# Loads of block tiles issued from ScalarE's queue instead of SyncE's, in an fp32 two-layer kernel built on seven-product block matmuls

## The reference

```python
# first layer: D_FF = 8192
m = rms_norm(h, mlp_pre_gain[l])
z = jnp.square(jax.nn.relu(jnp.einsum("bsd,df->bsf", m, w_up[l])))
z = jnp.einsum("bsf,fd->bsd", z, w_down[l])
h = h + rms_norm(z, mlp_post_gain[l])
...
# second layer: D_FF_2 = 5632
h2 = rmsnorm(x, g_ffn)
gu = h2 @ w_gu
x = x + (jax.nn.silu(gu[..., :D_FF_2]) * gu[..., D_FF_2:]) @ w_down
```

## Time and profile before

| what | value |
|---|---|
| median of 3 runs | 2445.73 us (2445.54 to 2446.38) |
| the profiled execution's own time | 2447.08 us |
| its span in the trace | 2445.2 us |
| PE busy | 2437.5 us (100%) |
| DVE busy | 1818.0 us (74%) |
| ACT busy | 1486.3 us (61%) |
| DMA queue of SP | 66.8% of 16 engines' time |
| granted TensorE clock | 1.0 in all of it |

### The profile page before, as it was taken

One profiled execution on the slowest core, in us unless ns is written; L12 is line 12 of the kernel. 1 busy time (PEld: TensorE's weight loads), 2 busy tenths in 40 slices (PEclk: granted clock), 3 DMA queues, 4 the chain that ended last, 5 costly groups with the idle time before them and its releaser, 6 DMA issues.

```text
span 2445.2 us, 28786 instructions
## 1 busy us (share of the span) xinstructions
PE 2437.5 (100%) x10849; PEld 2017.9 (83%) x10849; DVE 1818.0 (74%) x1967; ACT 1486.3 (61%) x1801; POOL 66.8 (3%) x78
## 2 busy tenths in 40 slices
PE   9999999999999999999999999999999999999999
PEld 8888888888888888888888888888888888888887
DVE  5888578878888887766577645546688888878874
ACT  6886557567467576556666555546666545564553
POOL 0110000000000000011100000000000000000000
PEclk9999999999999999999999999999999999999999
DMA  8997667768678577576756666667767666675755
GB/s 283 267 262 219 197 197 206 230 201 228 215 207 243 189 230 208 153 219 211 228 179 200 196 202 199 202 193 215 242 189 217 212 198 216 197 223 182 229 175 172
DMA packets 348562, 515.41 MB, mean 211 GB/s; under 512 B 113840, under 2 KB 114152, under 8 KB 348168
## 3 DMA queue, kind: packets, MB, share of 16 engines
q1 hardware_dynamic: 343592, 496.63, 66.8%
q0 software_dynamic: 4688, 16.93, 3.2%
q10 hardware_dynamic: 144, 0.01, 0.0%
HBM read 476.52 MB, written 4.47 MB: 197 GB/s over the span
## 4 chain that ended last, share of the span: by engine, by line
PE 92%; DVE 4%; ACT 2%; issue 1%; DMA 1%; SPq 0%; POOL 0%; DVEq 0%; ACTq 0%; POOLq 0%
PE acc L601 15%; PE acc L603 15%; PE acc L602 15%; PE acc L766 12%; PE acc L767 12%; PE acc L768 12%; DVE w_lo L1554 2%; PE acc L754 1%; PE acc L755 1%; PE acc L753 1%; PE tp L754 1%; PE tp L755 1%; PE tp L753 1%; PE sc L753 1%; PE sc L754 1%
## 5 line engine op out<-in xcount | busy, mean ns | idle before, releaser
L1554 DVE TENSOR_TENSOR w_lo<-raw,w_hi 128x1024 fp32r<-128x1024 f32 x776 | 941.6, 1222 | 496.4 <-ACT w_hi L970 490.8
L970 ACT ACTIVATE w_hi<-raw 128x1024 fp32r<-128x1024 f32 x776 | 814.9, 1057 | 723.9 <-PE acc L603 378.8
L601 PE MATMUL acc<-w_lo,a_hi 128*128 128x512 f32 x1216 | 476.9, 392 | 0.7 <-issue 0.7
L603 PE MATMUL acc<-w_hi,a_lo 128*128 128x512 f32 x1216 | 473.8, 390 | 0.0
L602 PE MATMUL acc<-w_hi,a_hi 128*128 128x512 f32 x1216 | 473.5, 389 | 0.0
L767 PE MATMUL acc<-w_hi,a_hi 128*128 128x512 f32 x816 | 317.6, 389 | 0.0
L766 PE MATMUL acc<-w_lo,a_hi 128*128 128x512 f32 x816 | 317.6, 389 | 0.0
L768 PE MATMUL acc<-w_hi,a_lo 128*128 128x512 f32 x816 | 317.6, 389 | 0.0
L970 ACT ACTIVATE w_hi<-quad_raw 128x1024 fp32r<-128x1024 f32 x196 | 207.7, 1060 | 112.1 <-PE acc L768 60.2
L601 PEld LDWEIGHTS acc<-w_lo,a_hi 128*128 128x128 f32 x1216 | 228.4, 188 | 48.0 <-issue 1.7
L603 PEld LDWEIGHTS acc<-w_hi,a_lo 128*128 128x128 f32 x1216 | 228.3, 188 | 47.9
(11 more groups left out here) (310 smaller groups left out, 2881.6 us busy)
## 6 DMA issues: line engine op xcount, KB each, us to landing
raw<-w_in_dram SPq DMA_DIRECT2D x272, 512.0 KB, 4.6
raw<-w_down_dram SPq DMA_DIRECT2D x172, 512.0 KB, 4.4
raw<-w_gu_dram SPq DMA_DIRECT2D x136, 512.0 KB, 4.5
raw<-w_up_dram SPq DMA_DIRECT2D x100, 512.0 KB, 4.5
raw<-w_out_dram SPq DMA_DIRECT2D x64, 512.0 KB, 4.4
quad_raw<-w_down_dram SPq DMA_DIRECT2D x44, 512.0 KB, 6.1
quad_raw<-w_gu_dram SPq DMA_DIRECT2D x40, 512.0 KB, 5.6
raw<-w_branch_dram SPq DMA_DIRECT2D x32, 512.0 KB, 4.1
```

Source lines behind the costliest of these rows:

```text
L601: nc.tensor.matmul(out, xh, wl, start=s == 0 and k == 0, stop=False)
L603: mm = nc.tensor.matmul(out, xl, wh, start=False, stop=s == n - 1 and k == KS - 1)
L970: nc.scalar.activation(w_hi[:, g % RING], src, ACT.Copy).then_inc(hi_ready, 1)
L1554: nc.vector.tensor_tensor(w_lo[:, g % RING], src, w_hi[:, g % RING].bitcast(F32), ALU.subtract).then_inc(lo_ready, 1)
```

## The change

The 112 loads of block tiles leave SP's program and go into ACT's, each behind the rounding of a slot of the pair that runs. For a following pair that starts at slot `G_PAIR`, tile 1 is issued 10 slots earlier (index 9 of the running pair), tile 0 nine earlier (index 10), tile 2 seven earlier (index 12) and tile 3 four earlier (index 15). The waits are the same semaphores and values, taken by ACT. Sources, tiles and sizes stay; the order of the tiles was 1, 0, 3, 2 and is 1, 0, 2, 3. SP keeps the plain loads and the transposes. The source function moves out of SP's program unchanged.

```diff
+LOAD_AT = {G_PAIR[name] + i: (tile, q) for q, name in enumerate(QUADS)
+           for tile, i in ((1, -10), (0, -9), (2, -7), (3, -4))}
...
         @block.sync
...
-            def load_block(q, tile, src):
-
-                if q == 0:
-                    sp.wait_ge(slot_used, G_MLP)
-                    sp.wait_ge(h_ready, NCH)
-                elif q == Q_FF:
-                    sp.wait_ge(slot_used, G_FF)
-                else:
-                    g, order = G_PAIR[QUADS[q - 1]], DOWN if "down" in QUADS[q - 1][0] else UP
-                    last = ("T2", "T3", "B21", "B22")[tile]
-                    sp.wait_ge(lo_ready, g + order.index(last) + 1)
-                    sp.wait_ge(quad_sum, 4 * q)
-                sp.dma_start(quad_raw[:, tile], src).then_inc(quad_in[tile], 16)
...
-                blocks = {6: 1, 8: 0, 10: 3, 11: 2}
...
                     load(pair_src(name, unit, s))
-                    if following in QUADS and k in blocks:
-                        tile = blocks[k]
-                        load_block(QUADS.index(following), tile, pair_src(following, tile % 2, tile // 2))
...
         @block.scalar
         def _(act):
+            def load_block(tile, q):
+
+                if q == 0:
+                    act.wait_ge(slot_used, G_MLP)
+                    act.wait_ge(h_ready, NCH)
+                elif q == Q_FF:
+                    act.wait_ge(slot_used, G_FF)
+                else:
+                    g, order = G_PAIR[QUADS[q - 1]], DOWN if "down" in QUADS[q - 1][0] else UP
+                    last = ("T2", "T3", "B21", "B22")[tile]
+                    act.wait_ge(lo_ready, g + order.index(last) + 1)
+                    act.wait_ge(quad_sum, 4 * q)
+                act.dma_start(quad_raw[:, tile], pair_src(QUADS[q], tile % 2, tile // 2)
+                              ).then_inc(quad_in[tile], 16)
...
                 nc.scalar.activation(w_hi[:, g % RING], src, ACT.Copy).then_inc(hi_ready, 1)
+                if g in LOAD_AT:
+                    load_block(*LOAD_AT[g])
```

More of the change, by code:

```diff
@@ L389, in tap_first, with pair_src @@
                                         cols[:, G_CBIAS + c:G_CBIAS + c + 1], ALU.mult, ALU.add)
+        def pair_src(name, unit, s):
+            stage, b, i = name
+            if stage == "up":
+                c0 = b * D + (2 * i + unit) * W
+                return w_up[:, slice(KS * s, KS * s + KS), c0:c0 + W]
+            if stage == "down":
+                c0 = (2 * i + unit) * W
+                return w_down[:, b * KT + KS * s:b * KT + KS * s + KS, c0:c0 + W]
+            if stage == "ff down":
+                c0 = (2 * i + unit) * W
+                return w_dn2[:, b * KT + KS * s:b * KT + KS * s + KS, c0:c0 + W]
+            c0 = unit * FF2 + b * D + i * W
+            return w_gu[:, slice(KS * s, KS * s + KS), c0:c0 + W]
         block = ctx.enter_context(nc.Block())
@@ L460, in _, with load_pair @@
                     load(w_out[:, ks(part * RING + s), c0:c0 + W])
-            def load_block(q, tile, src):
-                if q == 0:
-                    sp.wait_ge(slot_used, G_MLP)
-                    sp.wait_ge(h_ready, NCH)
-                elif q == Q_FF:
-                    sp.wait_ge(slot_used, G_FF)
-                else:
-                    g, order = G_PAIR[QUADS[q - 1]], DOWN if "down" in QUADS[q - 1][0] else UP
-                    last = ("T2", "T3", "B21", "B22")[tile]
-                    sp.wait_ge(lo_ready, g + order.index(last) + 1)
-                    sp.wait_ge(quad_sum, 4 * q)
-                sp.dma_start(quad_raw[:, tile], src).then_inc(quad_in[tile], 16)
[L476 to L491, removed]
-                blocks = {6: 1, 8: 0, 10: 3, 11: 2}
+            def load_pair(name, turns):
                 if name in QUADS:
@@ L498, in load_pair @@
                     steps = [(unit, s) for unit in range(2) for s in range(SPU)]
-                    blocks = {k + 3: tile for k, tile in blocks.items()}
                 for k, (unit, s) in enumerate(steps):
@@ L503, in load_pair @@
                     load(pair_src(name, unit, s))
-                    if following in QUADS and k in blocks:
-                        tile = blocks[k]
-                        load_block(QUADS.index(following), tile, pair_src(following, tile % 2, tile // 2))
             mlp_pairs = [(stage, b, i) for b in range(MLP_BLOCKS) for stage in ("up", "down")
                          for i in range(2)]
-            for name, following in zip(mlp_pairs, mlp_pairs[1:] + [None]):
+            for name in mlp_pairs:
                 stage, b, i = name
@@ L517, in _ @@
                     turns = {3: [("ff", x + 2)], 8: [("ff", x + 3)]}
-                load_pair(name, following, turns)
+                load_pair(name, turns)
             for v in range(3 * NCH):
@@ L550, in _ @@
                         [("ff", b, j) for j in range(FF_PAIRS[b])] + [("ff down", b, i) for i in range(2)]]
-            for name, following in zip(ff_pairs, ff_pairs[1:-1]):
+            for name in ff_pairs:
                 stage, b, j = name
```

## The result

| | us, median (lowest to highest) |
|---|---|
| before | 2446.06 (2445.54 to 2446.41, 4 runs) |
| after | 2476.06 (2468.89 to 2483.97, 4 runs) |

The ratio is 1.0122, with an interval of 1.0110 to 1.0134: slower by 30.0 us. The forecast was 2447.5, at most 2449.3 at the end of its range. The prediction was wrong. The profiled execution is the fastest of the four after, 2468.89 us, with a span of 2467.1; the time to explain in the trace is 2467.1 - 2445.2 = 21.9 us.

What follows compares the result with a forecast made beforehand. PE was taken as the bound, busy 2437.5 of 2445.2 us. Two tight pairs at +0.9 us, all else 0, gave +1.8 us on 2445.73: 2447.5 us, with an 8-in-10 range of 2444.9 to 2449.3.

Steps and rivals of the forecast that it cites:

- The bound, the tight pairs, the path: PE bounds; in two `ff down` pairs (0.15 us slack) a later transpose delays join, remainder and PE's matmul one for one.
- SP loses 112 issues: SP's queue: without the block load ahead, transposes go out up to 0.5 us earlier in each of two pairs.
- ACT gains 112 issues: ACT's queue, four issues a pair at about 0.42 us: taken as 0, upper end 0.5 us in all.
- ACT's new waits: ACT waiting for the T4 sum ahead of tile 1: taken as 0, at most under one DVE operation, 1.22 us.
- Rival B: Block-load issues on ACT held about 4 us by full engines: 90 us slower, 2535 us; chance 0.05.
- The tiles arrive at other times: Block tiles' landing: tile 3 has 11.3 us, slowest landing 8.9, 2.4 us left, so no new wait.
- The first pair: Join at 364.35, tile 3 moving beside its transposes: taken as 0, estimated -1 to +1 us.
- Tile 2 moves ahead of the transposes' end: Tile 2 goes out during the transposes: -0.5 to +1.5 us per tight pair with the earlier issue, +0.9 taken.
- In these two pairs, and only in them with certainty: Only in `("ff down", 0, 0)` and `("ff down", 1, 0)` does a later transpose certainly delay PE, one for one.
- Rival C: Transposes delayed by tiles 0 and 2 in three pairs, 3.0 us each: +7.5 us, 2453.2 us; chance 0.04.
- The 2.0 us that I drew from it: Cost for the two tight pairs if tile 2 is served within the transposes by turns: 2 x (1.5 - 0.5).

Runs made afterwards that it cites:

- experiment 8: The kernel before, all on SP's queue, with tile 0 issued behind the transposes instead of ahead of them in the second layer's pairs: 2444.64 us, ratio 0.9993.
- experiments 3: The kernel before, with ACT issuing block loads only in pairs where SP issues no transposes (48 loads): 2446.45 us, ratio 1.0000.
- experiment 6: The kernel after, but only tiles 0, 1 and 3 on ACT, tile 2 on SP at its old place: 2446.00 us, ratio 0.9998.
- Experiment 2: The kernel before, all block loads on SP's queue, with tile 2 issued ahead of the second layer's transposes: 2450.87 us, ratio 1.0018.
- 5: The kernel after, but only tile 2 issued by ACT, tiles 0, 1 and 3 on SP at their old places: 2473.33 us, ratio 1.0115.
- experiment 9: The kernel before, but GpSimd issues tile 2 after ACT's rounding of slot index 11, other tiles stay on SP: 2473.80 us, ratio 1.0112.
- 7: The kernel after, with tile 2 in two 256 KB halves, one behind slot index 12, one behind index 16: 2459.48 us, ratio 1.0048.
- 10: The kernel after, with tile 2 as two DMAs in rows of 1 KB instead of 2 KB, both behind slot index 12: 2468.39 us, ratio 1.0083.
- experiment 1: The kernel after, with tile 2 issued by ACT behind slot index 16, behind the join, instead of index 12: 2449.66 us, ratio 1.0014.

## Why the prediction was wrong

- **The bound, the tight pairs, the path.** Right. The chain runs through the same transposes, join, remainder and late matmul, and in the trace of experiment 8 PE's waits of the second layer go when the transposes come sooner.
- **SP loses 112 issues.** Right: its wait of 124.8 us for T4 sums is gone, and the transposes go out 0.33 us sooner (0 to 0.5 was said).
- **ACT gains 112 issues; ACT's new waits.** Right at nothing: 0.38 us each, beside the rounding; experiments 3 and 6 put 48 and 84 of them on ACT for -0.1 and -0.4 us. Rival B, an issue held by full engines, did not come.
- **The tiles arrive at other times.** DVE idled 3.7 us in all ahead of the 112 block sums (in its row above), so no new wait of size for a tile. The slowest tile took 10.9 us to land, not 8.9, still inside the 11.3 us that the step counted.
- **The first pair.** Right at nothing: its join waited 2.4 us, not 3.17. The last 144 packets of tile 3 lie beside these transposes and spread their packets only from 4.0 to 4.6 us.
- **The step that failed: "Tile 2 moves ahead of the transposes' end".** It named the right collision and put -0.5 to +1.5 us on it, +0.9 taken. Measured, the join is 4.2 us later in that pair. The bound of 1.5 us came from tile 2's bytes at 347 GB/s, which supposes that the engines move transposes and a foreign copy together as fast as plain loads. They moved 169 to 182 GB/s, and the transposes' landing lagged 1.4 us more behind their last packet, which the sum did not have either. Experiment 2 shows that the same bytes in one queue cost 1.6 and 2.6 us in the two pairs: the bound was near for another kernel.
- **"In these two pairs, and only in them with certainty".** That followed from the small price. The joins of the nine second-layer pairs with transposes now wait 2.4, 4.0, 5.4, 5.9, 0.9, 4.5, 5.0, 6.0 and 3.8 us. Seven of these waits are longer than the slack of 2.8 us, and behind those seven, and only those, two starts of PE lie 0.38 us or more further apart than 0.227 (tight pair: up to 4.0); the first layer loses 5.2 us besides. Behind a wait of 3.84 us PE then ran at the lower clock for 3 to 4 us, some 1.7 us more, which no term of the sum held.
- **Rival C** had the right sign and cause, transposes delayed by more than one tile, but at 3.0 us for each of three places it gave 2453.2, and 0.04.

On the Trainium skill: its page *DMA: Bandwidth & Descriptors*, "Queues, rings and completion order", says that an engine takes turns between queues a packet at a time. The windows agree in that packets of both queues come in the same 2 us (410 and 117); they do not show the turns themselves. The 2.0 us that I drew from it did not hold, since the rule says nothing of the rate that is left; here it was 169 GB/s.

**What stays open.** Why transposes and a foreign copy together move so little, and why the transposes then land so late behind their last packet, is not settled. The runs show that it takes a second queue (2 against 5), whichever (9), that it takes transposes (plain loads in two queues moved 337 GB/s), that a smaller copy costs less time (7), and that the count of foreign packets is not the price (10). Why tile 3 does no harm beside the first pair's transposes (3) was not tried. Of the 3 us left in experiment 1 about half is the first pair's; the rest lies in the first layer, where tiles 0 and 1 are beside transposes as in experiment 6, which has 2.3 us there and makes it up in the second. Of the 30.0 us between the medians, 21.9 are in the trace of the fastest run; the other runs have lower granted clocks (2468.89 us at 0.999, 2472.66 at 0.998, 2479.47 at 0.996, 2483.97 at 0.994), which fits waits that let the clock fall, and was not traced.

## What to carry to other kernels

Moving loads to another engine's queue also takes away an order that one queue gave for nothing: here it kept block tiles out of the time in which transposes were in flight. Before such a move, look for a small, urgent transfer (a DMA transpose above all) that will then share the engines, and keep the moved copies out of its time; a different place (experiment 1) saves what a different engine (experiment 9) does not. Price a collision of a transpose with another queue's copy by a measurement, not by bytes at the full rate, and compare the delay with the slack of every place where it happens, not of the tightest alone.

## What the runs showed of the hardware

- DMA transposes beside a 512 KB copy from another queue: 205 small packets a us instead of 1043, the copy 58 instead of 170, together 169 GB/s in one stretch of 2 us (182 over their common time), with the engines shown as busy as before. Plain loads in the same two queues moved 337 GB/s together.
- The two transposes had landed 0.5 us after their last packet with nothing beside them, and 1.9 to 2.7 us after it with the copy beside them (second layer, nine pairs).
- A DMA issue on ACT's queue runs beside the activation ahead of it: 0.38 us, starting 0.08 us into it.
- SP's issue of two transposes took 5.58 us when a 512 KB tile stood right ahead of them and 3.22 us without that tile (experiment 8). It does not show the state of SP's queue alone: in after, where that tile lies in ACT's queue, it took 5.29 us.
- A single wait of PE of 3.84 us was followed by 3 to 4 us at the lower clock (matmuls 0.43 us apart instead of 0.23).
